# Diff attention begun inside the last value slot: turns in other banks, half a slot of products between the first scores

## What is computed

```python
proj = h @ w_in                                     # 1024 x 3072: queries, keys, values
q = apply_partial_rope(rms_norm(q, q_g), cos, sin) * (d ** -0.5)      # 16 halves of 64
k = apply_partial_rope(rms_norm(k, k_g), cos, sin)
s = jnp.einsum('bqhcd,bkhcd->bhcqk', qb, k)         # 8 heads, c = 0, 1
p = jax.nn.softmax(jnp.where(mask, s, -jnp.inf), axis=-1)
a = p[:, :, 0] - lam * p[:, :, 1]
o = rms_norm(jnp.einsum('bhqk,bkhe->bqhe', a, v), subln_g) * (1.0 - lam_init)
return o.reshape(B, S, H * DIFF_V_DIM) @ w_out
```

## Time and profile before

| | |
|---|---|
| median of 3 runs | 1496.18 us (1495.94 to 1496.65) |
| profiled execution, time | 1497.59 us |
| profiled execution, span | 1495.7 us |
| granted clock of TensorE, mean | 0.972 of full speed |
| busy share of the span | PE 94%, DVE 60%, ACT 42%, POOL 4% |
| mean DMA rate | 139 GB/s |

### The profile page before, as it was taken

The page is one execution under the profiler, slowest core; times in us unless marked ns, Lnnn a source line. Parts: engine busy times, 40 slices in busy tenths (PEclk is TensorE's granted clock), DMA queues, the critical chain, the costliest instruction groups (busy, mean ns, idle before and its releaser), DMA issues.

```text
span 1495.7 us, 21793 instructions
## 1 busy us (share of the span) xinstructions
PE 1400.3 (94%) x8596; PEld 1217.4 (81%) x8596; DVE 900.1 (60%) x1579; ACT 622.3 (42%) x946; POOL 61.2 (4%) x45
## 2 busy tenths in 40 slices
PE   5999999989999897899999898789999998999998
PEld 4885999689999656799999677679999777889997
DVE  6277467586777404477676567565654567475554
ACT  2232221353433337554343556554333457454331
POOL 0002000000000002000000002000000033000000
PEclk8999999999999899999999899999999999999999
DMA  6423101365554041455564153094551312376520
GB/s 221 163 89 113 57 2 57 98 213 177 189 187 139 32 137 66 131 198 179 197 196 141 60 214 121 1 345 166 207 211 70 113 63 87 118 277 225 185 96 29
DMA packets 110796, 208.11 MB, mean 139 GB/s; under 512 B 3808, under 2 KB 53088, under 8 KB 110208
## 3 DMA queue, kind: packets, MB, share of 16 engines
q1 hardware_dynamic: 110720, 207.06, 39.9%
HBM read 205.99 MB, written 1.05 MB: 138 GB/s over the span
## 4 chain that ended last, share of the span: by engine, by line
PE 84%; DVE 8%; ACT 6%; issue 2%; DMA 0%; SPq 0%; DVEq 0%; ACTq 0%
PE ps L820 19%; PE ps L740 12%; PE ps L806 10%; PE ps L801 10%; PE ps L796 9%; PE ps L1034 4%; PE ps L718 3%; PE ps L856 3%; PE ps L867 2%; ACT Ah L1403 1%; PE ps L693 1%; DVE arena L2370 1%; PE ps L1266 1%; PE ps L1157 1%; PE ps L931 1%
## 5 line engine op out<-in xcount | busy, mean ns | idle before, releaser
L1413 ACT CAST Ah<-ringA 128x2048 fp32r<-128x2048 f32 x76 | 145.1, 1909 | 280.4 <-PE ps L806 266.0
L1981 DVE TENSOR_TENSOR Al<-ringA,Ah 128x2048 fp32r<-128x2048 f32 x76 | 174.2, 2292 | 85.4 <-ACT Ah L1413 85.1
L796 PE MATMUL ps<-hTh,Ah 128*128 128x256 f32 x1216 | 169.5, 281 | 5.6 <-DVE hTl L1966 5.1
L801 PE MATMUL ps<-hTl,Ah 128*128 128x256 f32 x1216 | 170.2, 282 | 0.6 <-DVE hTl L1966 0.6
L796 PEld LDWEIGHTS ps<-hTh,Ah 128*128 128x128 f32 x1216 | 159.3, 188 | 12.0 <-issue 5.8
L806 PE MATMUL ps<-hTh,Al 128*128 128x256 f32 x1216 | 168.7, 281 | 0.0
L1988 DVE TENSOR_TENSOR Bl<-ringB,Bh 128x1024 fp32r<-128x1024 f32 (+1 forms) x76 | 127.0, 1671 | 55.1 <-ACT Bh L1422 55.1
L801 PEld LDWEIGHTS ps<-hTl,Ah 128*128 128x128 f32 x1216 | 155.7, 189 | 1.1 <-DVE hTl L1966 1.0
L1422 ACT CAST Bh<-ringB 128x1024 fp32r<-128x1024 f32 (+1 forms) x76 | 107.5, 1414 | 113.2 <-PE ps L820 110.3
L806 PEld LDWEIGHTS ps<-hTh,Al 128*128 128x128 f32 x1216 | 154.3, 189 | 0.0
L820 PE MATMUL ps<-Bh,hidh 128*128 128x512 f32 x432 | 135.1, 394 | 5.2 <-issue 3.6
(11 more groups left out here) (355 smaller groups left out, 2013.2 us busy)
## 6 DMA issues: line engine op xcount, KB each, us to landing
ringA<-in_ffn_w_in SPq DMA_DIRECT2D x44, 1024.0 KB, 7.1
ringA<-in_mlp_w SPq DMA_DIRECT2D x32, 1024.0 KB, 7.5
ringB<-in_mlp_w SPq DMA_DIRECT2D x32, 1024.0 KB, 6.8
ringB<-in_ffn_w_out SPq DMA_DIRECT2D x44, 512.0 KB, 4.1
ringA<-in_diff_w_in SPq DMA_DIRECT2D x12, 1024.0 KB, 6.6
ringA<-in_dsa_w_in SPq DMA_DIRECT2D x8, 1024.0 KB, 6.3
ringA<-in_w_k SPq DMA_DIRECT2D x4, 1024.0 KB, 8.4
ringA<-in_w_r SPq DMA_DIRECT2D x4, 1024.0 KB, 6.3
```

What stands on the lines that cost most here:

```text
L796: mm(o, Ah[:, half, k * T + j * P:k * T + j * P + P], hTh[:, k, :], start=(k == 0), stop=False)
L801: mm(o, Ah[:, half, k * T + j * P:k * T + j * P + P], hTl[:, k, :], start=False, stop=False)
L1413: nc.scalar.copy(a_split(w, Ah, half), a_half(w, ap, half)).then_inc(ah_rdy, 1)
L1981: V.tensor_tensor(a_split(w, Al, half), a_half(w, (a_at[w] + par) % 2, half), a_split(w, Ah, half).bitcast(F32), ALU.subtract).then_inc(al ...
```

## The change

- **Banks of the turns.** Queries are turned into banks 0 to 3, keys into banks 0, 2, 3 and 5 (`turn_pairs`), outside the job counting: new semaphores `dt` and `dte` join TensorE and ScalarE (`diff_turned`). The jobs q2 and k2 are gone.
- **Slot 5** no longer uses job banks but banks 1 and 6 (`V5`). TensorE does two of its first half's three parts, then turns the keys, then does the third part. Its second half becomes three parts of 8 matmuls (`values`): behind score 3, behind scores 6 and 7, behind scores 8 and 9. ScalarE copies the result out behind `turned_p(2)`, and `turn(4)` waits for those copies.
- **The first heads** turn into bank 7 (0 to 3) and put out into bank 0 (0 to 2), with waits for the head before in place of the one two before.
- **ScalarE's queue.** The root for the keys and slot 5's first cast change places. wo2's casts move from before the attention to before and behind the split of the turned output. The squares of head 7 go to VectorE.
- **VectorE's queue.** The keys' squares move ahead of slot 4's second rest, and the later rests one place back. The rests of wo2 come from GpSimd, which has none of them now.

Where the lines of the two differ in number, L740 is L752 in the new kernel for `split_slot`, and slot 5's matmuls are L1248.

```diff
@@ -482,10 +483,13 @@
         c = Carve(8192)
         d_p = c(6144).rearrange("p (j t n) -> p j t n", j=3, t=2)
-        d_soft = c(3456)
+        d_pr = c(1536).rearrange("p (j n) -> p j n", j=4)
         c.at = 18432
         d_rt = c(1024)
         d_lam = c(8)
+        d_soft = (c(1152).rearrange("p (j n) -> p j n", j=3), d_pr,
+                  c(768).rearrange("p (j n) -> p j n", j=2))
+        V5 = (1, 6)
@@ -557,6 +563,12 @@
+        def turn_bank(h0, h, diff):
+            return 7 if diff and h in (0, 2) else 6 + (h0 + h) % 2
+
+        def out_bank(h0, h, diff):
+            return 0 if diff and h < 3 else (h0 + h) % 2
@@ -1150,9 +1162,11 @@
+                    if diff and h == 4:
+                        pe.wait_ge(job_out, J["din2"][0] + 4)
                     if h0 + h >= 2:
-                        pe.wait_ge(pre["pte"], h0 + h - 1)
-                    b = 6 + (h0 + h) % 2
+                        pe.wait_ge(pre["pte"], h0 + h - 1 + (diff and h in (1, 2, 3)))
+                    b = turn_bank(h0, h, diff)
@@ -1161,8 +1175,8 @@
-                        pe.wait_ge(pre["ov"], h0 + h - 1)
-                    b = (h0 + h) % 2
+                        pe.wait_ge(pre["ov"], h0 + h - 1 + (diff and h in (1, 2)))
+                    b = out_bank(h0, h, diff)
@@ -1172,12 +1186,16 @@
                 for u in range(3 * per):
                     scores(u)
+                    if diff and u == 3:
+                        values(0)
                 for h in range(heads):
                     turn(h)
                     if h:
                         out(h - 1)
                     for u in range(per * (h + 3), min(per * (h + 4), 16)):
                         scores(u)
+                    if diff and h < 2:
+                        values(h + 1)
                 out(heads - 1)
...
@@ -1206,22 +1224,70 @@
 
 
             turn16("n2")
-            for s in range(6):
+            def last_job(b):
+                return max(j for j in range(J["din2"][0] + 2) if bank(j) == b)
+
+            def turn_pairs(j, banks):
+
+                for i, b in enumerate(banks):
+                    for k in (2 * i, 2 * i + 1):
+                        for t in range(NT):
+                            o = (k % 2) * T + t * P
+                            last = nc.tensor.transpose(ps[:, b, o:o + P],
+                                                       d_p[:, j, t, k * P:(k + 1) * P], ident)
+                    last.then_inc(pre["dt"], 1)
+
+            def value_part(half, left, right, first=False, last=None):
+
+                a = a_at["din"] + 5
+                for t in range(NT):
+                    if first and t == 1:
+                        pe.wait_ge(job_out, last_job(V5[1]) + 1)
+                    for k in range(4 * half, 4 * half + 4):
+                        o = (k % 4) * 512
+                        ins = mm(ps[:, V5[t], :], left[:, k, t * P:(t + 1) * P],
+                                 right[:, half, o:o + 512], start=(first and k == 0),
+                                 stop=(last is job_rdy and k == KT - 1))
+                    if last is job_rdy:
+                        ins.then_inc(job_rdy, 1)
+                if last is a_used:
+                    ins.then_inc(a_used, 1)
+
+            def values(part):
+
+                n = 2 * SPLIT[a_at["din"] + 5] + 1
+                if part == 0:
+                    pe.wait_ge(ah_rdy, n + 1)
+                    value_part(1, hTh, Ah)
+                elif part == 1:
+                    value_part(1, hTl, Ah)
+                else:
+                    pe.wait_ge(al_rdy, n + 1)
+                    value_part(1, hTh, Al, last=job_rdy)
+
+            for s in range(5):
                 split_jobs(a_at["din"] + s, in_job("din", s), "n2" if s == 0 else None)
                 if s == 3:
                     pe.wait_ge(pre["dq"], 1)
-                    turn_blocks(J["q2"][0], [((lambda t, k=k: d_p[:, 0, t, k * P:(k + 1) * P]), P)
-                                             for k in range(8)])
+                    turn_pairs(0, (0, 1, 2, 3))
+            n = 2 * SPLIT[a_at["din"] + 5]
+            pe.wait_ge(pre["dte"], 4)
+            pe.wait_ge(ah_rdy, n + 1)
+            value_part(0, hTh, Ah, first=True)
+            value_part(0, hTl, Ah)
             pe.wait_ge(pre["src"], 2)
-            turn_blocks(J["k2"][0], [((lambda t, k=k: d_p[:, 1, t, k * P:(k + 1) * P]), P)
-                                     for k in range(8)])
-            pe.wait_ge(job_out, J["k2"][0] + 4)
+            pe.wait_ge(job_out, last_job(5) + 1)
+            turn_pairs(1, (0, 2, 3, 5))
+            pe.wait_ge(al_rdy, n + 1)
+            value_part(0, hTh, Al, last=a_used)
+            pe.wait_ge(job_out, J["din2"][0] + 2)
+            pe.wait_ge(pre["dte"], 8)
 
             def half(ap, u):
                 return ap[64 * (u % 2):64 * (u % 2) + 64, u // 2, :]
 
             attend(1, lambda u: d_QZ[:, u, :], lambda u: KT8[:, u // 2, :],
-                   lambda t, h: d_p[:, 2, t, h * P:(h + 1) * P], P, d_soft)
+                   lambda t, h: d_p[:, 2, t, h * P:(h + 1) * P], P, d_soft, values)
             turn16("o2")
             out_proj(2)
             turn16("nm0")
...
@@ -1638,6 +1704,11 @@
                        scale=-1.0, accum_out=sm[:, 1:2]).then_inc(pre["e"], 1)
                     if diff and u % 2 and u >= 3:
                         turned_p(u // 2 - 1)
+                        if u == 7:
+                            for t in range(NT):
+                                act.wait_ge(job_rdy, J["din2"][0] + 3 + t)
+                                scaled(d_p[:, 2, t, 512:D], ps[:, V5[t], :], t
+                                       ).then_inc(job_out, 1)
                         if u >= 7:
                             squares(u // 2 - 3)
                     if not diff and u:
@@ -1645,9 +1716,10 @@
                 turned_p(16 // per - 1)
                 prime(ACT.Sqrt)
                 if diff:
-                    for h in range(5, 8):
+                    for h in range(5, 7):
                         ins = squares(h)
                     link(ins)
+                    act.wait_ge(pre["sq7"], 1)
 
             turned("n1", "g1_mix", "g_kv")
             late_norm("n1")
@@ -1710,27 +1782,37 @@
             round_slot(a_at["din"], 1)
             late_norm("n2")
             act.wait_ge(rs_rdy, LATE["n2"])
-            for s in range(6):
+            def diff_turned(n, b, *copies):
+
+                act.wait_ge(pre["dt"], n)
+                for f in copies:
+                    last = f(ps[:, b, :])
+                last.then_inc(pre["dte"], 1)
+
+            for s in range(5):
                 a = a_at["din"] + s + 1
+                if s == 4:
+                    head_root("dk", 1)
                 round_slot(a, 0)
                 if s == 2:
                     head_root("dq", 0)
                 elif s == 4:
-                    head_root("dk", 1)
                     act.wait_ge(pre["src2"], 1)
                     A_(d_lam[:, 2:4], d_lam[:, 0:2], ACT.Exp).then_inc(pre["osd"], 1)
                 for t in range(NT):
                     job(in_job("din", s) + t, lambda p: scaled(
                         d_p[:, s // 2, t, (s % 2) * 512:(s % 2) * 512 + 512], p, t))
-                if s < 5:
-                    round_slot(a, 1)
+                round_slot(a, 1)
                 if s == 3:
-                    turned_queries(lambda i, *f: job(J["q2"][0] + i, *f), d_QZ, col("dqk", 0), 1)
-            turned_keys(J["k2"][0])
-            round_slot(a_at["wo2"], 1)
+                    turned_queries(lambda i, *f: diff_turned(1 + i, i, *f), d_QZ, col("dqk", 0), 1)
+            for i, b in enumerate((0, 2, 3, 5)):
+                diff_turned(5 + i, b, lambda p: nc.scalar.copy(
+                    KT8[:, 2 * i:2 * i + 2, :].rearrange("p k t -> p (k t)"), p))
             attend(1, d_soft)
             A_(st[:, 40:56], st[:, 24:40], ACT.Sqrt, bias=eps, scale=0.5 / HD).then_inc(pre["osd"], 1)
+            round_slot(a_at["wo2"], 0)
             turned_split("o2", "sub")
+            round_slot(a_at["wo2"], 1)
             for half in range(2):
                 round_slot(a_at["wo2"] + 1, half)
             ffn_start("mlp0", 0)
@@ -1867,9 +1949,6 @@
                 rest_slot(a_at["wo1"], half)
             pool.wait_ge(x_done, 2 * MI["ffn1"] + 2)
             empty_halves(d_QZ, 1)
-            pool.wait_ge(pre["src"], 2)
-            for half in range(2):
-                rest_slot(a_at["wo2"], half)
             pool.wait_ge(x_done, 2 * MI["mlp0"] + 2)
             empty_halves(s_QZ, 2)
             for s in (3, 4):
@@ -2527,19 +2606,25 @@
             dve.wait_ge(pre["gt"], 1)
             rope2(d_p[:, 0], H, d_rt, gains=0, done=pre["dq"])
             rest_slot(a_at["din"] + 4, 0)
-            rest_slot(a_at["din"] + 4, 1)
             dve.wait_ge(job_out, J["din"][0] + 8)
             head_squares(d_p[:, 1], 1, d_sq)
```

(14 more changed lines are left out.)

11 lines of the change are left out of this document (7 added, 4 removed).

## The result

The changed kernel takes **1482.69 us** (median; 1477.8 to 1484.5) against 1495.94 (1491.39 to 1496.65) for the kernel before on the same chip: a ratio of 0.9909, 95% interval 0.9891 to 0.9927, so 13.6 us less, give or take 2.7. The profiled execution took 1483.59 us (span 1481.7; before 1497.59 and 1495.7).

What follows compares the result with a forecast made beforehand. TensorE, holding 84% of the chain, was taken as the bound. Earlier first score 12.4, less 1.8 for value parts, plus 0.6 tail gave 11.2 us off 1496.18: 1485.0 us, range 1482.8 to 1488.8.

Steps and rivals of the forecast that it cites:

- Queries into other banks: Diff attention stage: slot 4's products follow the query turns at 888.0 and end at 899.2 instead of 904.42.
- The keys: Before the first score: rotated keys ready at 902.5, 0.4 us ahead of need at 902.9; first score 12.4 us earlier.
- the third rival: Before the first score: VectorE's chain to the rotated keys still ends at 915.6; 1497.7 us, no change; chance 0.03.
- The attention: First score to last combine: three value parts moved in take back 1.8 of 12.4 us; last combine 10.6 us earlier.
- the hold: First combine: GpSimd's rest of wo2 holds VectorE's second operation for 2.45 us; this goes when the rests leave GpSimd.
- the switches: Attention: changes between value parts and fp32 scores, bounded by 0 and 0.3 us for each of seven, taken as 0.
- the first rival: First combine: the hold stays without GpSimd's rests and TensorE loses 1.3 us; 1486.3 us; chance 0.06.
- The tail: Last turned copy to root: VectorE squares the eighth head, so the distance of 3.78 us falls by 0.6.
- the stage's sum: Query turns to out-projection: 12.4 - 1.8 + 0.6 = 11.2 us less.
- Rests of wo2 and mlp0's load: Around the out-projection: wo2's rests stay hidden; mlp0's first load moves to about 949.5, hidden by 5 us before its cast.
- From the out-projection on every distance unchanged: Behind the stage: a sign of being right, all distances the same, only 11 us earlier.
- The rival by the clock: From 888 to 920 us: mixed short bursts drop TensorE to 1.2 GHz, up to 32 us more, 1517; chance 0.03.

Runs made afterwards that it cites:

- a_order: Changed kernel with VectorE's order of before (both rests ahead of keys' squares and rotation) and ScalarE's root order taken back: 1494.53 us, ratio to before 0.9993.
- a_front: Changed kernel with the three value parts ahead of the first score instead of between the first scores and turns: 1485.81 us, ratio to before 0.9943.
- b_rests: Kernel before with only GpSimd's two rests of wo2 moved to VectorE: 1491.56 us, ratio to before 0.9976.
- a_shift: Changed kernel with eight more products, results overwritten, some 35 us ahead of the query turns: 1485.94 us, ratio to before 0.9928.
- a_hold: Changed kernel with the first rest of wo2 back on GpSimd, its cast ahead of the attention: 1485.74 us, ratio to before 0.9941.
- b_queries: Kernel before with only the turned queries put into banks 0 to 3, with semaphores of their own: 1489.10 us, ratio to before 0.9956.
- b_three: Kernel before with wo2's rests on VectorE, queries in banks 0 to 3, and keys' squares, sums and root put forward; slot 5 unsplit: 1486.66 us, ratio 0.9948.
- r_before: Kernel before run once more, unchanged: 1495.51 us, ratio to before 1.0003.
- r_after: Changed kernel run once more, unchanged: 1482.07 us, ratio to before 0.9924.
- a_sq7: Changed kernel with the last head's squares back on ScalarE: 1481.54 us, ratio to before 0.9923.
- b_shift: Kernel before with eight more products, results overwritten, some 35 us ahead of the query turns: 1499.24 us, ratio to before 1.0024.

## Why the prediction was right, and where it was wrong

**Queries into other banks: right.** Slot 4 at 887.88 and slot 5 at 899.07 against 888.0 and 899.2.

**The keys: right, with less to spare than I wrote.** The key turns begin at 902.74, and the row of their weight load says that they wait 0.25 us for VectorE's last rotation (L2500): nothing is left of the 0.4. The text named this the tightest place, and a_order shows what it carries. a_order comes near the third rival (the keys come no earlier, 1497.7, no change): its keys are 5.2 us earlier than before and not 13.5, and the low clock behind them takes more, 1494.53. But the way there leads through three queues, not through VectorE's own durations.

**The attention: right in sum.** First score 12.67 us earlier (forecast 12.4), third turn to last combine 12.68 us (12.9), last combine 11.28 us earlier (10.6): the parts and their copies took back 1.39 and not 1.8. The runs give the pieces of this 1.39, up to the last turn: 5.53 us for the parts (first score in a_front), less the hold (2.29), less what the place between the scores hides (1.92), and 0.07 for the two value copies, which I had at 1.4 (first score to last turn: 23.72 us in b_rests without them, 23.79 in a_front with them). A part between scores takes 2.05 us of TensorE (908.82 to 910.88, the other two alike) and not 1.87: some 0.2 a part for the switches, which I bounded by 0 and 0.3 each and took at 0. One reading in this sum doesn't follow: VectorE at 2.92 us a head from 925.0 is ready for the last combine at 933.8 and not at 932.6, behind the 933.2 that I took. The last combine came at 932.52 and had waited 0.41 us for ScalarE, so ScalarE was the later one, as I had it.

**The hold: right.** 2.29 us in before. In the changed kernel one rest on GpSimd costs 1.98 up to the last turn, where the first rival had 1.3.

**The tail: right where the clock rises, and lost where it stays low.** I took the root to stand 0.6 us nearer to the last turned copy. In before the squares are the last to come there: VectorE's last scaled output ends at 947.77, ScalarE's last square at 949.31, and the root starts at 949.43.

```profile
947.16 0.61 DVE L2346 TENSOR_SCALAR xn<-ps,st 128x128 f32<-128x128 f32 x2 [0.23 <-PE ps L1169]
...
949.02 0.29 ACT L1623 ACTIVATE ringB<-xn 128x128 f32<-128x128 f32 x1
```

In a_front, a_shift and a_hold the distance is 0.6 shorter, as forecast. In the changed kernel's own profile it is 3.78 us again (934.73 to 938.51): TensorE's last outputs run near the low level, so the last scaled output ends at 937.87, VectorE's squares at 938.41, and the root waits for them. The last turn, too, takes 0.90 us instead of 0.55. From last turn to out-projection that makes 6.84 us against 6.55, 0.9 more than forecast; at the higher clock of the three other kernels it is 6.25. I had taken before's clock of 1.00 at this place for granted; in the 2.5 us from the last turn on b_queries, b_three and r_before have 0.50, 0.57 and 0.62. The last turn takes 0.90 us in all eight profiles that start from the changed kernel, and in the six from before 0.55 in three and 0.64 to 0.90 in the others; whether the change brings the low clock there stays open.

**Luck in the stage's sum.** First score 0.27 us better, attention 0.41 better, tail 0.9 worse: the 11.05 against 11.2 is as close as it is because they cancel.

**Rests of wo2 and mlp0's load: right.** SP issues the load at 950.24 (949.5), the cast takes it at 961.18 (961.9) and has waited for TensorE alone:

```profile
961.18 1.91 ACT L1479 CAST Ah<-ringA 128x2048 fp32r<-128x2048 f32 x1 [3.59 <-PE ps L752]
```

**"From the out-projection on every distance unchanged": the step that failed.** It took one profiled execution for the kernel, and so put the term for the clock outside the stage at nothing, in the sum and in the range. Behind the stage that execution had 544.08 us, and the changed kernel's first one 541.07; other executions of the two have 542.91 and 543.78. Over the four profiles with the changed stage (changed, r_after, a_shift, a_sq7) the two distances have means of 54.2 and 542.0, over the three of before (before, r_before, b_shift) 66.0 and 543.6: 13.4 us less together, near what the medians have. 11.75 of them are the stage. That the last 1.6 are more than chance is not shown by so few profiles, and stays open; over all unfilled profiles the means behind the stage are 542.4 for the seven that start from the changed kernel and 542.8 for the six from before. The range should have had this term: the three times of before that I had lay within 0.7 us of each other, and I read them as the spread. Over all its 80 runs the kernel before took 1491.05 to 1492.05 us in 22 and 1493.63 to 1498.80 in 58; of the changed kernel's 11 runs four took 1477.69 to 1478.36 and seven 1480.62 to 1486.84, so a median of a few runs jumps by several us. The means of all these runs are 13.2 us apart. With 3 us for the term the range would have begun near 1480. The mechanism and its 11 us stand as they were.

**The rival by the clock: out.** From 887 to 920 us the granted clock is 1.00, with value parts, scores and turns mixed in it.

## What to carry to other kernels

Judge a local change by the distance between two instructions of the limiting engine, one ahead of it and one behind; the span mixes it with what the clock does elsewhere, and here that is more than 5 us for the same code. Put the second cut where the clock is the same in both kernels: 0.6 us of clock at the end of the stage hid a third of what a_front measures. When work is moved forward in one queue, follow the chain through every queue that it passes (rest, cast, copy, root), since a delay in one of them comes back in the next: one order of rests was worth 4 us by durations and 11 in the run, 6.5 of them TensorE's waits and most of the rest the low clock behind them. Products put between the first scores of an attention hid 1.9 of 5.5 us here, and the rest lay on the path.

## What the hardware showed that I had not expected

- The same program, executed again, has its low-clock stretches elsewhere and of another length: 880.62 and 886.22 us to the same instruction, without a difference in its work. Between two cuts where the clock is the same it repeats to 0.03 us (47.54 to 47.57 in five profiles).
- Filling two waits of over 3 us kept the clock at 1.00 behind each of them, and did not shorten the kernel by anything that its time shows.
- GpSimd's rest held one VectorE operation for 2.45 and 2.74 us, while beside the same two rests ten operations with one input in PSUM, or with one input only, began and took their usual time.
